# The embedding's product and norm made inside the feed-forward's gate and up stage, and its gated sum made tile by tile

## The reference, cut to what matters

```
h = h + rms_norm(merged @ w_out[i], ln_post_mix[i])

f = rms_norm(h, ln_pre_ffn[i])
f = (jax.nn.silu(f @ w_ffn_gate[i]) * (f @ w_ffn_up[i])) @ w_ffn_down[i]
h = h + rms_norm(f, ln_post_ffn[i])

e = rms_norm(p[i].astype(h.dtype) @ w_ple[i], ln_ple[i])
h = h + jax.nn.sigmoid(h @ w_ple_gate[i]) * e
```

## Time and profile before

| | us |
|---|---|
| median of 3 runs | 2610.16 |
| lowest and highest | 2607.94 and 2615.74 |
| the profiled execution's own time | 2611.23 |
| its span, first to last instruction | 2609.4 |
| TensorE busy | 2308.0 (88%) |
| VectorE busy | 975.9 (37%) |
| ScalarE busy | 503.6 (19%) |
| mean granted TensorE clock | 0.944 of full speed |

### The profile page before, as it was taken

How to read it: one execution, slowest core, us unless ns; L and a number is a source line. 1 busy time by engine, 2 the same in 40 slices (tenths; PEclk the granted TensorE clock), 3 DMA queues, 4 the chain that set the end, 5 groups by cost and what they waited for, 6 DMA issues and landing times. The chain is left out here.

```text
span 2609.4 us, 32536 instructions
## 1 busy us (share of the span) xinstructions
PE 2308.0 (88%) x13329; PEld 1593.3 (61%) x13329; DVE 975.9 (37%) x2007; ACT 503.6 (19%) x972; POOL 74.0 (3%) x79
## 2 busy tenths in 40 slices
PE   7999878898999689999787979877959999879996
PEld 6888777787888544454674445433437567745553
DVE  1466134312000259995575231100031455234232
ACT  0133411101000120012321021000022666121111
POOL 0000022102000000000000001000010000000000
PEclk9999989998999789999887989999979999989998
DMA  8443463146642412564101339999852222479995
GB/s 251 145 131 118 151 215 98 49 147 260 194 151 80 152 46 86 183 202 158 49 1 41 137 113 374 399 397 409 304 190 86 71 81 75 170 306 398 391 397 207
DMA packets 239090, 483.71 MB, mean 185 GB/s; under 512 B 13234, under 2 KB 192484, under 8 KB 209636
## 3 DMA queue, kind: packets, MB, share of 16 engines
q1 hardware_dynamic: 218304, 439.36, 47.3%
q0 software_dynamic: 6480, 23.60, 2.4%
q10 hardware_dynamic: 14164, 18.76, 2.2%
HBM read 454.94 MB, written 26.74 MB: 185 GB/s over the span
## 5 line engine op out<-in xcount | busy, mean ns | idle before, releaser
L1897 PE MATMUL bank<-hn,weights 128*128 128x512 f32 x640 | 280.0, 598 | 2.3 <-ACT hn L403 2.3
L1897 PEld LDWEIGHTS bank<-hn,weights 128*128 128x128 f32 x640 | 121.7, 191 | 153.4 <-issue 152.4
L1971 DVE SCALAR_TENSOR_TENSOR conv_sum<-mixer_then_weights_ahead,vec,conv_sum 128x572 f32<-128x572 f32 x240 | 175.0, 823 | 0.0
L569 PE MATMUL bank<-u,weights 128*128 128x256 f32 x768 | 170.8, 379 | 0.9 <-PEq L192 0.9
L3499 PE MATMUL bank<-hn,weights 128*128 128x512 f32 (+1 forms) x512 | 169.2, 488 | 0.0
L569 PEld LDWEIGHTS bank<-u,weights 128*128 128x128 f32 x768 | 144.8, 190 | 24.1 <-issue 5.4
L1530 PE MATMUL bank<-u,weights 128*128 128x256 f32 x704 | 154.5, 383 | 1.0 <-DVE u L384 1.0
L1530 PEld LDWEIGHTS bank<-u,weights 128*128 128x128 f32 x704 | 135.4, 192 | 19.9 <-issue 1.1
L3499 PEld LDWEIGHTS bank<-hn,weights 128*128 128x128 f32 x512 | 96.0, 190 | 65.3 <-issue 58.4
L3650 DVE SCALAR_TENSOR_TENSOR x_both<-bank,mod_later,x_both 128x256 f32<-128x256 f32 x144 | 63.1, 480 | 163.4 <-PE bank L2732 161.1
L2354 PE MATMUL bank<-mixer_then_weights_ahead,weights 128*128 128x512 f32 x256 | 111.4, 595 | 0.0
(11 more groups left out here) (569 smaller groups left out, 3283.3 us busy)
## 6 DMA issues: line engine op xcount, KB each, us to landing
weights<-in_mod_w SPq DMA_DIRECT2D x48, 1024.0 KB, 7.8
weights<-in_w_in SPq DMA_DIRECT2D x36, 1024.0 KB, 5.2
weights<-in_moe_w_gate SPq DMA_DIRECT2D x36, 1024.0 KB, 21.3
weights<-in_moe_w_up SPq DMA_DIRECT2D x36, 1024.0 KB, 22.1
weights<-in_moe_w_down SPq DMA_DIRECT2D x36, 1024.0 KB, 20.8
weights<-in_ab_w_in SPq DMA_DIRECT2D x20, 1024.0 KB, 5.4
mixer_then_weights_ahead<-in_moe_w_gate SPq DMA_DIRECT2D x20, 1024.0 KB, 29.6
mixer_then_weights_ahead<-in_moe_w_up SPq DMA_DIRECT2D x20, 1024.0 KB, 30.7
```

What stands on the lines that cost most here:

```text
L569: last = pe.matmul(bank(n), unit[:, k, m * P:(m + 1) * P], x(k), start=k == 0, stop=k == ktiles - 1)
L1897: last = pe.matmul(tile_bank(n)[:, :], unit[:, k, lane * P:(lane + 1) * P], hn[:, k, :], start=k == 0, stop=k == DC - 1)
L1971: ins = dve.scalar_tensor_tensor(s, x, w, s, ALU.mult, ALU.add)
```

## The change

1. **`gated_hidden` also makes `e`.** At its start ScalarE issues the load of `p` into `zg`. Tiles are counted from 0. Behind tile 3 TensorE transposes `p` into bank 6 (4 matmuls) and VectorE copies it. Behind tiles 8 and 9 TensorE makes 4 tiles each of the `w_ple` product, in banks 4 and 5 in turn; ScalarE copies each into `zg` and VectorE squares it. Behind tile 11 TensorE sums the squares (32 matmuls of 32 columns of weights), VectorE and ScalarE make the inverse root between them, and behind tile 13 TensorE spreads it into bank 4 and VectorE scales the 8 tiles (`e`, still in `zg`).
2. **The plan of weights.** `w_ple` is unit 8 of the gate and up units, ahead of the gate unit of tiles 8 and 9; its slot counts as free after 11 tiles. It is gone from behind the down units, and so `w_ple_gate` follows the down units directly.
3. **The stages behind the norm of the feed-forward** (load, turn, `w_ple` product, norm, gate product, product and sum) become one, `gated_add`. The norm's sum goes to `zg` tiles 0 to 7 (`hz`) and not to `h`. ScalarE's Sigmoid of each gate tile is followed by VectorE's product with `e` and its sum with `hz` into `h`, tile by tile.

```
 def gated_hidden(kit, x, T, widths, hidden, zero, norm, ple):
+    first = 2 * PLE_PAIR
+    done.insert(first, first + 3)
+    FOURTH = T // 4
+        total, root = kit.bank[6][:, 0:FOURTH], kit.bank[4][:, 0:T]
...
+                def turn_p():
+                    pe.wait_ge(p_loaded, 16)
+                    for j in range(2):
+                        for t in range(2):
+                            last = pe.transpose(kit.bank[6][:, (2 * j + t) * P:(2 * j + t + 1) * P], ple.tokens[:, t, j * P:(j + 1) * P], kit.c("ident"))
+                    last.then_inc(p_turned, 1)
+
+                def ple_tile(j):
+                    pe.wait_ge(p_copied, 1)
+                    if j >= 2:
+                        pe.wait_ge(ple_copied, j - 1)
+                    for k in range(2):
+                        last = pe.matmul(kit.bank[4 + j % 2][:, 0:T], ple_unit[:, k, j * P:(j + 1) * P], ple.turned[:, k, :], start=k == 0, stop=k == 1)
+                    last.then_inc(ple_ready, 1)
+
+                def ple_sums():
+                    for c in range(DC):
+                        pe.wait_ge(ple_squared, c + 1)
+                        for g in range(4):
+                            last = pe.matmul(total[32 * g:32 * g + 32, :], kit.c("ones")[:, 0:32], ple.squares[:, c, g * FOURTH:(g + 1) * FOURTH],
+                                             start=c == 0, stop=c == DC - 1)
+                    last.then_inc(ple_summed, 1)
+
+                def ple_spread_roots():
+                    pe.wait_ge(ple_copied, DC)
+                    pe.wait_ge(ple_inverted, 1)
+                    for g in range(4):
+                        last = pe.matmul(root[:, g * FOURTH:(g + 1) * FOURTH], kit.c("ident")[:, 32 * g:32 * g + 1].broadcast_to([P, P]),
+                                         rstd[:, :], start=True, stop=True)
+                    last.then_inc(ple_spread, 1)
+
                 for w in widths:
+                    if n == first:
+                        ple_unit = feed.arrive(pe, (2, D))
                     gate = feed.arrive(pe, (DC, w))
                     up = feed.arrive(pe, (DC, w))
...
                         last.then_inc(pair_ready, 1)
+                        if n == first - 5:
+                            turn_p()
+                        if n in (first, first + 1):
+                            for j in range(4):
+                                ple_tile(4 * (n - first) + j)
+                        if n == first + 3:
+                            ple_sums()
+                        if n == first + 5:
+                            ple_spread_roots()
...
             def _(act):
+                act.dma_start(ple.tokens, ple.source.rearrange("(t p) d -> p t d", p=P)).then_inc(p_loaded, 16)
...
+                    if n in (first, first + 1):
+                        for j in range(4 * (n - first), 4 * (n - first) + 4):
+                            act.wait_ge(ple_ready, j + 1)
+                            act.copy(ple.out[:, j, :], kit.bank[4 + j % 2][:, 0:T]).then_inc(ple_copied, 1)
+                    if n == first + 3:
+                        act.wait_ge(ple_mean, 1)
+                        act.activation(rstd[:, :], rstd[:, :], ACT.Sqrt).then_inc(ple_root, 1)
...
             def _(dve):
...
+                    if n == first - 5:
+                        dve.wait_ge(p_turned, 1)
+                        dve.tensor_copy(ple.turned.rearrange("p j t -> p (j t)"), kit.bank[6][:, :]).then_inc(p_copied, 1)
+                    if n in (first, first + 1):
+                        for j in range(4 * (n - first), 4 * (n - first) + 4):
+                            dve.wait_ge(ple_copied, j + 1)
+                            dve.tensor_tensor(ple.squares[:, j, :], ple.out[:, j, :], ple.out[:, j, :], ALU.mult).then_inc(ple_squared, 1)
+                    if n == first + 3:
+                        dve.wait_ge(ple_summed, 1)
+                        dve.tensor_scalar(rstd[:, :], total, 1.0 / D, EPS, ALU.mult, ALU.add).then_inc(ple_mean, 1)
+                        dve.wait_ge(ple_root, 1)
+                        dve.reciprocal(rstd[:, :], rstd[:, :]).then_inc(ple_inverted, 1)
+                    if n == first + 5:
+                        dve.wait_ge(ple_spread, 1)
+                        for c in range(DC):
+                            dve.scalar_tensor_tensor(ple.out[:, c, :], ple.out[:, c, :], kit.col("ln_ple", c), root, ALU.mult, ALU.mult)
+
+def gated_add(kit, x, gate, e, out):
+    sync, tensor, drain = project_programs(kit, lambda k: x[:, k, :], DC, SEQ, [WIDE] * 4,
+                                           lambda act, s, n, ps: act.activation(gate[:, n, :], ps, ACT.Sigmoid))
...
+            for n in range(DC):
+                dve.wait_ge(evacuated, n + 1)
+                dve.tensor_tensor(gate[:, n, :], gate[:, n, :], e[:, n, :], ALU.mult).then_inc(multiplied, 1)
+                dve.wait_ge(multiplied, n + 1)
+                dve.tensor_tensor(out[:, n, :], x[:, n, :], gate[:, n, :], ALU.add)
...
+            ple = Embedding(source=inp["p"][0, 0], tokens=zg[:, 0:2, :], turned=zg[:, 2:4, :], squares=zg[:, 16:24, :], out=zg[:, 8:16, :])
+            gated_hidden(kit, ux, SEQ, [WIDE] * 11, hidden, ob[:, 0:4, :].rearrange("p c t -> p (c t)"), norm, ple)
             project_down(kit, lambda k: hidden[:, k, :], SEQ, [2] * 11, lambda e, s, m, ps: e.tensor_copy(ya[:, m, :], ps))
-        rmsnorm(kit, ya, [(slice(0, SEQ), lambda c: h[:, c, :], lambda c: kit.col("ln_post_ffn", c), None, lambda c: h[:, c, :])])
-            load_turned(kit, inp["p"][0, 0], lambda c: pair(pt[:, c:c + 2, :]), 2, "p")
-            project(kit, lambda k: pt[:, k, :], 2, SEQ, [1024], lambda e, s, n, ps: e.tensor_copy(ob[:, n, :], ps))
-            rmsnorm(kit, ob, [(slice(0, SEQ), lambda c: ya[:, c, :], lambda c: kit.col("ln_ple", c), None, None)])
-            project(kit, lambda k: h[:, k, :], DC, SEQ, [WIDE] * 4,
-                    lambda e, s, n, ps: e.activation(u[:, n, :], ps, ACT.Sigmoid), "scalar")
-            vector_only(kit, add_ple)
+        hz = zg[:, 0:8, :]
+        rmsnorm(kit, ya, [(slice(0, SEQ), lambda c: hz[:, c, :], lambda c: kit.col("ln_post_ffn", c), None, lambda c: h[:, c, :])])
+        gated_add(kit, hz, u, ple.out, h)
...
+    hidden_units.insert(2 * PLE_PAIR, kpn(inp["w_ple"][0]))
+    feed.plan(1, 23, lambda i, j: hidden_units[j])
     feed.plan(1, 11, lambda i, j: down[:, 2 * j:2 * j + 2, :])
-    feed.plan(1, 1, lambda i, j: kpn(inp["w_ple"][0]))
     feed.plan(1, 4, wide(kpn(inp["w_ple_gate"][0])))
```

More of the change, by code:

```diff
@@ L14 @@
 from contextlib import ExitStack, contextmanager
+from dataclasses import dataclass
 import numpy as np
@@ L1488, in _, with gated_hidden @@
                 dve.tensor_copy(out[:, h0 + 2:h0 + 4, :], kit.bank[5][:, :].rearrange("p (a b) -> p a b", a=2)).then_inc(v_copied, 1)
-def gated_hidden(kit, x, T, widths, hidden, zero, norm):
+PLE_PAIR = 4
+def gated_hidden(kit, x, T, widths, hidden, zero, norm, ple):
     nc = kit.nc
@@ L1498, in gated_hidden @@
         done += [m, m]
+    first = 2 * PLE_PAIR
+    done.insert(first, first + 3)
+    FOURTH = T // 4
     with ExitStack() as mem:
         sg = mem.enter_context(kit.sb("silu_gate", [P, 2, T]))
[L1501 to L1502 removed]
+        rstd = mem.enter_context(kit.sb("rstd", [P, FOURTH]))
+        total, root = kit.bank[6][:, 0:FOURTH], kit.bank[4][:, 0:T]
+        with stage(nc, "pair_ready", "silu_ready", "hidden_ready", "zeroed", "p_loaded", "p_turned", "p_copied", "ple_ready", "ple_copied", "ple_squared",
+                   "ple_summed", "ple_mean", "ple_root", "ple_inverted", "ple_spread", *norm.SIGNALS) as (
+                block, pair_ready, silu_ready, hidden_ready, zeroed, p_loaded, p_turned, p_copied, ple_ready, ple_copied, ple_squared,
+                ple_summed, ple_mean, ple_root, ple_inverted, ple_spread, *norm_signals):
             norm.bind(*norm_signals)
@@ new lines, in gated_add, with _ @@
+def gated_add(kit, x, gate, e, out):
+    sync, tensor, drain = project_programs(kit, lambda k: x[:, k, :], DC, SEQ, [WIDE] * 4,
+                                           lambda act, s, n, ps: act.activation(gate[:, n, :], ps, ACT.Sigmoid))
+    with stage(kit.nc, "tiles_ready", "evacuated", "multiplied", "step") as (block, ready, evacuated, multiplied, step):
+        @block.sync
+        def _(sp):
+            sync(sp, ready)
+        @block.tensor
+        def _(pe):
+            tensor(pe, ready, evacuated)
+        @block.scalar
+        def _(act):
+            drain(act, ready, evacuated, step)
+        @block.vector
+        def _(dve):
+            for n in range(DC):
[3 more added lines that the diff above has]
+                dve.tensor_tensor(out[:, n, :], x[:, n, :], gate[:, n, :], ALU.add)
@@ L1551, in rows_of @@
+@dataclass
+class Embedding:
+    source: object
+    tokens: object
+    turned: object
+    squares: object
+    out: object
 def rows_of(name, ap):
@@ L1617, in turn_rest @@
     turn(kit, groups)
```

(21 more changed lines are left out.)

8 lines of the change are left out of this document (removed).

## The result

| | before | changed |
|---|---|---|
| median, us | 2611.84 (7 runs) | 2594.74 (7 runs) |
| lowest and highest | 2607.94 to 2617.72 | 2592.16 to 2601.66 |
| profiled execution, us | 2611.23 | 2594.51 |
| its span | 2609.4 | 2592.6 |
| mean granted clock | 0.944 | 0.945 |

Seven runs of each kernel were compared; the median of 2610.16 in the table before was that of the first three of the kernel before. The ratio is 0.9939, with a 95% interval of 0.9925 to 0.9954: 17.1 us between the medians, 16.7 between the two profiled executions; forecast were 2594 and 16.5 us less. TensorE's busy time is nearly what it was (2308.0 before, 2307.2 now): no work went, a gap did.

A forecast was written before the change was run, and what follows sets the result against it. The prediction took TensorE's work plus its gaps, in a chain of stages, as the bound: -23.0 - 4.1 + 10.6 = -16.5 us, so 2594 us against the 2610.16 median, 0.6% faster, range 2588 to 2600.

The forecast's parts named there:

- What goes: Between feed-forward norm and gate product: load, turn, product and norm stages leave, so the gate product starts 23.0 us earlier.
- the prediction's own sign: At the gate product's start: expected 13.7 us after the down products; later than 14 us would mean the prediction was wrong.
- The tail: Behind the last Sigmoid: two 256-element VectorE instructions replace two wide ones, ending 4.1 us sooner.
- TensorE's added work: In the gate and up stage: transposes, `w_ple` product, sums and spread add 10.6 us, bounds 10.5 and 12.8.
- Waits: In the gate and up stage: no added waits on banks, engines or weights; two late-asked units have margins 5.6 and 3.0 us.
- The clock: At the gate product's first tile: the same 3.0 us half-clock loss as before, so it cancels; next norm's gain taken as 0.
- The sum of the region: From feed-forward norm to next norm, plus the stage's added work: -23.0 - 4.1 + 10.6 = -16.5 us.
- first rival: Gate product's first tile at full speed (-3.0) and part of the next norm (-1 to -2.9): 2589 us; chance 0.13.
- The late load and the banks: In the gate and up stage: tile 8's load late 4.2 us, banks 2.4, together 6.6, so 2600 us; chance 0.12.
- The lost lead: Before tiles 8 and 12: late units hold TensorE 12.6 and 17.9 us, together 30.5, so 2624 us; chance 0.03.
- The gain only in part: TensorE's added pieces cost about 20 us instead of 10.6, or later stages give back: 2603 us; chance 0.04.

The follow-up runs named there:

- both experiments on it: Tail undone, and tail alone: the kernel before given only the change's tile-by-tile tail; tail alone measured 2606.51 us, ratio 0.9959.
- busy norm: The change plus useless matmuls in TensorE's gaps of the norm behind the down products only: 2591.18 us, ratio 0.9914 to the kernel before.
- short lead: The change with the embedding weights' slot free after 12 tiles, not 11, so one up unit is asked for later: 2599.32 us, ratio 0.9944.
- one bank: The change with all eight tiles of the embedding's product in bank 4 instead of two banks in turn: 2597.28 us, ratio 0.9946.
- change once more: The change unaltered, run again as partner for other kernels: 2594.11 us, ratio 0.9912 to the kernel before.
- tail undone: The change with the former tail: Sigmoids, then one product and one sum over all eight tiles: 2597.15 us, ratio 0.9944.
- earlier place: The change with the embedding's product behind tiles 6 and 7 instead of 8 and 9: 2598.95 us, ratio 0.9941.
- busy norms: The change plus useless matmuls in TensorE's gaps of all norms but the first and last: 2580.01 us, ratio 0.9861.
- in the gap: The change with the embedding's transposes and product moved into the norm behind the mixer's output product, plus four useless matmuls there: 2593.37 us, ratio 0.9919.

## Why the prediction was right, step by step

- **What goes**, 23.0 us: measured 23.0. The gate product starts 0.31 us after the norm of the feed-forward ends (867.26), 0.33 was said. By the prediction's own sign (a gate product that starts later than 14 us after the down products) something was wrong: it starts 14.1 us after them, for 13.7 said. The 0.4 us are in the norm ahead of it, under the clock below, not in the move.
- **The tail**, 4.1 us: measured 4.15 in the changed kernel's rows (3.25 us from the last Sigmoid's end to the next sums, 7.40 before) and in the gap of both experiments on it.
- **TensorE's added work**, 10.6 us with bounds 10.5 and 12.8: measured 9.5, below the lower bound. The term was mis-sized: I took sums and spread from norms at 1.55 and 1.57 us, where the clock is in part at half; amid a full stage, at 1.00, they cost 1.04 and 0.84, each with 0.1 ahead of it. Transposes 0.44 and product 6.92 were as said. The stage lasts 164.2 us, for 165 said.
- **Waits**: none, as said. The margins of the two weight loads were 6.6 and 2.4 us, for 5.6 and 3.0. That the change needs such margins is shown by the two kernels in which one was gone.
- **The clock**: the gate product's first Sigmoid starts 6.3 us after the product's start, 6.5 before: the loss cancels, as said. The busy norm shows that it is the clock. What I took as zero: the norm behind the down products took 0.4 us longer, its sums now wholly at half clock (1.94 in place of 1.55), and the stage's first tile ended 0.25 us later. Neither goes with the change in every profile: the short lead and the one bank have 1.54 us in the same norm, and the change once more has 9.48 us to its first Silu, 9.50 before.
- The sum of the region: -23.0 - 4.1 + 9.5 + 0.4 + 0.2 - 0.1 = -17.1, and the row of the next norm's sums moved by 17.1 us (918.80 to 901.72). Behind it 0.4 us came back. The forecast of -16.5 is so near partly by luck: the added work was put 1.1 us too dear, and half of that went again to the clock's scatter. And the median's scatter of several us would have hidden an error of this size.
- **Rivals.** *The clock*: the gate product's first tile was not at full speed in the change. In the next norm it can be: in the change once more its sums and spread take 2.51 and 1.28 us, 3.64 and 2.08 in the first profile, so there a part of the first rival came true. It was not the shorter gap alone: with the tail undone, behind a gap of 7.82 us, the spread takes 1.16. *The late load and the banks*: the feed's lead was enough, and two banks hold nothing up. *The lost lead* is no story: it cost 7 us with the shorter lead and 1.8 at the earlier place, never the 16.5 that would have decided. *The gain only in part*: the pieces cost less than their rows, not more.

## What to carry to other kernels

Work that depends on nothing late was worth taking out of the chain of stages even though its new place was full: it cost its bare stream there (9.5 us), and in the chain it cost every stage's start, drain and handover as well (23.0 us). Before inserting it, count for each later weight unit what lead is left, against the landing time at that moment, with its neighbours' traffic; and price a long stand at more than its length: behind one of 5.7 us the clock was at half, behind those of 1.8 and 2.1 us it was not. Gaps of TensorE in a chain of norms, as the one of 6.4 us ahead of the gate product, cost twice for the same reason, and useless matmuls in them bought 14 us here, nearly as much as the change itself.

## What the runs showed of the hardware that I had not expected

- A stand of 5.7 us of TensorE in a full stage brought the granted clock to 0.50 for 4 us behind it: 2.1 us more on two tiles. Stands of 1.8 us (earlier place, busy norms) and 2.1 us (in the gap) left it at 1.00.
- A 1 MB load landed in 5.4 us with POOL's queue quiet, and one took 29.3 us amid POOL's 25 transfers of 0.5 MB.
- Table loads: Sqrt's at 705.13 takes 1.28 us, and its ACTIVATE starts at 706.43, 0.02 us behind its end. The Trainium skill ("ScalarE: Activation LUTs", What ACT_TABLE_LOAD costs) gives 2.66 us for a switch with its drain; this trace shows 1.3, with no more than 0.02 us between the ACTIVATE ahead (705.11) and the load.
- One bank's turn (four records, ScalarE's copy, the next tile) is 1.65 us against 0.86 with two, though the copy is 0.37.
